# Turning the gated blocks of a SwiGLU as 32x32 squares, with the moves between quadrants on SyncE's DMA queue

## The chip, the cores and the metric

One core of one Trainium2 chip runs the whole kernel. The metric is the device time of one execution, in microseconds (us).

## The reference

A decoder trunk of two layers over x of 256 rows and 2048 columns, all float32. Each layer adds a token mixer (layer 0: chunked gated linear attention, layer 1: forgetting softmax attention), and then a SwiGLU:

```python
h = rms_norm(x, norm_ffn[i])
x = x + (jax.nn.silu(h @ w_gate[i]) * (h @ w_up[i])) @ w_down[i]    # w_gate, w_up: 2048 x 5632, w_down: 5632 x 2048
```

The change lies in the two SwiGLU stages.

## The kernel before, in words

**Products.** Every large product is float32 made of float32r products: a weight chunk (256 rows x 512 columns, 512 KB, as 128 partitions x 1024) is split into a high and a low part, and TensorE adds hi x hi, lo x hi and hi x lo (three matmuls of 512 columns for each 128x128 block of the left side). A chunk takes 12 matmuls.

**The path of a chunk.** SyncE loads it into `raw` (L332, four slots); it waits until the chunk four before has its low part. ScalarE makes `w_hi` (L766) once the chunk has landed and TensorE is through with the chunk four before; VectorE makes `w_lo` = raw - w_hi (L1244); TensorE waits for `w_lo` and multiplies. The four engines each have their own program, with the order written out by hand; semaphores count chunks.

**Gate and up.** `DFF` = 5632 is worked in 11 tiles (`FT`) of 512 columns. A plain tile i (i = 0, 1, 2 and 10) takes 8 chunks of `w_gate` (n = 0 to 7) and then 8 of `w_up` (n = 8 to 15). Tiles 3 to 9 (`gate_up`, from `GU0` to `GU1`) have 16 chunks as well, and one pair of chunks in them (n = 6 and 7) goes through a seven-product scheme: VectorE makes differences of the raw chunks, ScalarE and VectorE split them, TensorE makes seven products for eight, and VectorE adds them up again (`g_sum`). ScalarE then makes the silu of the gate product into `act`; early in tile i+1, after the third chunk, VectorE multiplies it with the up product into `stage` (`hidden`, `hidden_joined`): a gated block, 128 partitions x 2 row blocks x 512.

**Turning a gated block.** The down projection needs it with its columns on the partitions. `swap_h` (L1295) does this with VectorE: 16 transposes (L1304), each from 32 partitions of `stage` to 32 partitions of `hraw` (`ht_raw` in the trace), with eight 32x32 squares in each, spread between the `w_lo` of the chunks n = 3 to 12. At n = 14 ScalarE copies `hraw` to `ht_hi` (L878) and VectorE makes `ht_lo` (L1313), both `turn_h`. For the first two blocks `sums` (L1323 to L1326) also forms sums of parts of `hraw` for the seven-product scheme of the down projection. The last block of a layer is turned in the first chunks of the down projection. The attention output tiles use `swap_h` as well, and go on doing so.

**Down.** Two passes of 44 chunks (`ORDER`), with four pairs in the seven-product scheme in each.

Of the kernel before, what the change touches and what calls it, by code (L numbers as in the profile page):

```python
# [37 lines left out]
P = 128  # L38
Q = 32
# [37 lines left out]
def build(nc, x, norm_mix, norm_ffn, gla_w_in, gla_w_g2, gla_b_g2, gla_o_gain, gla_w_o,  # L77
# [59 lines left out]

    def gate_chunk(c_up, i):
        return Lin(c_up + 2 * CH * i) if isinstance(i, int) else Lin(c_up, 2 * CH, i)
# [7 lines left out]
    with ctx:  # L147
# [102 lines left out]
        xt_half = 4 * KC * S // 2  # L250
        g_hi = at("gate_diff_hi", [P, 4, N], 36 * K, F32R)
# [61 lines left out]
        diff_part = sem("first_differences_made")  # L313
        p1_gate, gate_sums, gate_joined, up_joined = (sem("first_gate_product_read"), sem("gate_sums_made"),
# [10 lines left out]
        @block.sync  # L325
        def _(sp):
            def load(src, row, col, c, j):

                slot = j % SLOTS

                wait(sp, lo_done, c + (j - SLOTS + 1))
                sp.dma_start(  # L332
                    raw[:, slot, :].rearrange("p (k n) -> p k n", n=N),
                    src[row:row + KC_CHUNK * P, bass.ds(col, N) if not isinstance(col, int) else slice(col, col + N)]
                    .rearrange("(k p) n -> p k n", p=P)).then_inc(landed[slot], 16)

            def project(src, col0, tiles, c0):

                with sp.Fori(0, tiles // 2) as i:
                    for j in range(2 * CH):  # L340
                        load(src, j % CH * KC_CHUNK * P, i * (2 * N) + (col0 + j // CH * N),
                             Lin(c0, 2 * CH, i), j)

            def swiglu(layer, c_up, c_down):
                plain = [("one", j // CH, j % CH) for j in range(2 * CH)]
                for i in range(FT):
                    for n, (kind, t, j) in enumerate(ORDER_GU if GU0 <= i < GU1 else plain):
                        load((w_gate, w_up)[t][layer], j * KC_CHUNK * P, i * N, gate_chunk(c_up, i), n)
                for i in range(DT // 2):
                    for n, (kind, t, j) in enumerate(ORDER):  # L350
                        load(w_down[layer], j * KC_CHUNK * P, i * (2 * N) + t * N, Lin(c_down + 2 * HCH * i), n)

            def load_x(h):
                s = slice(h * KC_CHUNK * P, (h + 1) * KC_CHUNK * P)
                sp.dma_start(xres[:, :, s], x[0, :, s].rearrange("(b p) n -> p b n", p=P)) \
                    .then_inc(x_landed[h], 16)

            x_before = {0: (0,), 1: (1,), 2: (2,), 3: (3,), 4: (4, 5), 5: (6,), 6: (7,)}
            for j in range(2 * CH):
                for h in x_before.get(j, ()):  # L360
                    load_x(h)
                load(gla_w_in[0], j % CH * KC_CHUNK * P, j // CH * N, Lin(C["gla_in"]), j)
            project(gla_w_in[0], 2 * N, 2 * QT + 2 * DT - 2, C["gla_in"] + 2 * CH)
            project(gla_w_o[0], 0, DT, C["gla_o"])
            swiglu(0, C["ffn0"], C["down0"])
            project(fox_w_in[0], 0, 3 * DT, C["fox_in"])
            project(fox_w_in[0], 3 * D + FH, DT, C["fox_in"] + 3 * DT * CH)
            project(fox_w_o[0], 0, DT, C["fox_o"])
            swiglu(1, C["ffn1"], C["down1"])
            for b in range(TB):  # L370
                sp.wait_ge(staged, G["ffn1"] + FT + DT + b)
                sp.dma_start(out[0, b * P:(b + 1) * P, (DT - 1) * N:DT * N], stage[:, b, :]).then_inc(last_stored, 16)
            sp.wait_ge(last_stored, 16 * TB)
# [378 lines left out]
        def _(ac):  # L752
# [122 lines left out]
            def turn_h(n, t):  # L875

                wait(ac, turned, n + 1)
                nc.scalar.activation(ht_hi[:, bass.ds(t.v * 4, 4), :] if t.reg is not None  # L878
                                     else ht_hi[:, 4 * t.base:4 * t.base + 4, :],
                                     hraw[:, :, :], ACT.Copy).then_inc(tp_hi, 1)  # L880
# [30 lines left out]
            def out_and_ffn(c_o, g_o, c_up, g_up, c_down, g_down, norm, first, first_turn, after):  # L911
# [6 lines left out]

                def silu(i):
                    count = i if isinstance(i, int) else 0  # L920
                    reg = i is not None and not isinstance(i, int)
                    wait(ac, chunk_used, Lin(c_up + CH, 2 * CH, i) if reg else Lin(c_up + (2 * count + 1) * CH))

                    wait(ac, staged, Lin(g_up, 1, i) if reg else Lin(g_up + count))
                    if i is None:
                        ac.wait_ge(rstd_ready, norm + 1)
                    for b in range(TB):
                        last = nc.scalar.activation(act[:, b, :], acc[:, 0, b, :], ACT.Silu,
                                                    scale=rstd[:, norm, b:b + 1])
                    last.then_inc(gate_done, 1)  # L930
# [3 lines left out]
                for i in range(1, 1 + SEVEN // 2):  # L934
                    cc = Lin(c_up + i * 2 * CH)
                    tile(cc, 0, None)
                    tile(cc, CH, lambda: silu(i), lambda: turn_h(Lin(g_up - 1 + i), Lin(i - 1)))
# [11 lines left out]
                gate_up(layer, c_up, GU0, lambda: silu_joined(GU0), lambda: turn_h(Lin(g_up - 1 + GU0), Lin(GU0 - 1)))  # L949
                with ac.Fori(GU0 + 1, GU1) as i:  # L950
                    gate_up(layer, c_up, i, lambda: silu_joined(i), lambda: turn_h(Lin(g_up - 1, 1, i), Lin(-1, 1, i)))
                for i in range(GU1, FT):
                    cc = Lin(c_up + i * 2 * CH)
                    tile(cc, 0, None)
                    tile(cc, CH, lambda: silu(i), lambda: turn_h(Lin(g_up - 1 + i), Lin(i - 1)))
                events = {(0, 10): lambda: turn_h(Lin(g_up + FT - 1), Lin(FT - 1))}
# [275 lines left out]
        def _(ve):  # L1232
# [76 lines left out]
            def turn_h(n, t):  # L1309
                wait(ve, turned, n + 1)  # L1310
                wait(ve, tp_hi, n + 1)
                s = bass.ds(t.v * 4, 4) if t.reg is not None else slice(4 * t.base, 4 * t.base + 4)
                nc.vector.tensor_tensor(ht_lo[:, s, :], hraw[:, :, :], ht_hi[:, s, :].bitcast(F32),  # L1313
                                        ALU.subtract).then_inc(tp_lo, 1)

            def sums(i):

                src = hraw[:, :, :].rearrange("p (j r) (b t) -> p j r b t", r=KC_CHUNK, t=P)
                a11, a12, a21, a22 = (src[:, :, r, b, :] for b in range(TB) for r in range(KC_CHUNK))
                dst = s_raw[i % (SEVEN // 2)]  # L1320
                if i >= SEVEN // 2:
                    ve.wait_ge(diff_used, down_step(i // (SEVEN // 2) - 1, DT // 2 - 1, SEVEN - 1) + 1)
                nc.vector.tensor_tensor(dst[:, :, 2, :], a11, a21, ALU.subtract)  # L1323
                link(nc.vector.tensor_tensor(dst[:, :, 0, :], a21, a22, ALU.add))
                link(nc.vector.tensor_tensor(dst[:, :, 1, :], dst[:, :, 0, :], a11, ALU.subtract))
                nc.vector.tensor_tensor(dst[:, :, 3, :], a12, dst[:, :, 1, :], ALU.subtract).then_inc(sum_raw, 1)  # L1326
# [27 lines left out]
            def gate_up(layer, c_up, i, hidden, turn, swap):  # L1354
# [4 lines left out]
                for n, (kind, t, j) in enumerate(ORDER_GU):  # L1359
# [26 lines left out]
                    if n in (3, 4, 5, 8, 9, 10, 11, 12):  # L1386
                        swap(2 * (n - 3) if n < 6 else 2 * (n - 5))
# [4 lines left out]
                    if n == 13:  # L1392
                        wait(ve, gate_sums, sums + 1)
# [98 lines left out]
            def out_and_ffn(c_o, g_o, c_up, g_up, c_down, g_down, m, norm, first, first_turn, saved):  # L1492
# [31 lines left out]
                def gate_swaps(n):  # L1524
                    return lambda j: swap_h(n, 2 * (j - 3), 2) if j >= 3 else None

                def up_swaps(n):
                    return lambda j: swap_h(n, 10 + 2 * j, 2) if j < 3 else None

                tile(Lin(c_up), 2 * CH, lambda: hidden(Lin(0)), swaps=gate_swaps(Lin(g_up)))  # L1530
                layer = norm // 2

                def turn_sums(n, i):
                    turn_h(n, Lin(i))
                    sums(layer * (SEVEN // 2) + i)

                tile(Lin(c_up), 3 * CH, None, lambda: turn_sums(Lin(g_up), 0), swaps=up_swaps(Lin(g_up)))
                x_sums_low(layer)
                for i in range(2, 1 + SEVEN // 2):
                    sums_lo(layer * (SEVEN // 2) + i - 2)  # L1540
                    n = Lin(g_up - 1 + i)
                    tile(Lin(c_up + i * 2 * CH), 0, lambda: hidden(Lin(i - 1)), swaps=gate_swaps(n))
                    tile(Lin(c_up + i * 2 * CH), CH, None, lambda: turn_sums(n, i - 1), swaps=up_swaps(n))
                sums_lo(layer * (SEVEN // 2) + SEVEN // 2 - 1)
                def hidden_joined(i):
# [9 lines left out]
                    for b in range(TB):  # L1555
# [5 lines left out]
                gate_up(layer, c_up, GU0, lambda: hidden(Lin(GU0 - 1)), lambda: turn_h(Lin(g_up - 1 + GU0), Lin(GU0 - 1)),  # L1561
                        lambda first: swap_h(Lin(g_up - 1 + GU0), first, 2))
                with ve.Fori(GU0 + 1, GU1) as i:
                    gate_up(layer, c_up, i, lambda: hidden_joined(i), lambda: turn_h(Lin(g_up - 1, 1, i), Lin(-1, 1, i)),
                            lambda first: swap_h(Lin(g_up - 1, 1, i), first, 2))
                for i in range(GU1, FT):
                    cc = Lin(c_up + 2 * CH * i)
                    n = Lin(g_up - 1 + i)
                    tile(cc, 0, lambda: hidden_joined(i) if i == GU1 else hidden(Lin(i - 1)), swaps=gate_swaps(n))
                    tile(cc, CH, None, lambda: turn_h(n, Lin(i - 1)), swaps=up_swaps(n))  # L1570
# [7 lines left out]
                swapped(g_up + FT - 1, 0, (3, 4, 5, 8))  # L1578
                events[0, 11] = lambda: turn_h(Lin(g_up + FT - 1), Lin(FT - 1))
# [500 lines left out]
```

## Time and profile before

| | |
|---|---|
| median of 3 runs | 2296.45 us (2296.32 to 2296.54) |
| profiled execution, its own time | 2296.2 us |
| its span, first to last instruction | 2294.5 us |
| TensorE matmul busy | 2287.3 us |
| VectorE busy | 1725.1 us (75%) |
| ScalarE busy | 1153.3 us (50%) |
| DMA engines, mean busy share by SyncE's queue | 63.7% |
| granted TensorE clock | 1.00 of full speed |

Busy is the time in which an engine runs at least one instruction. For matmuls it is modelled, and neighbouring ones overlap: a matmul of 512 columns is shown with 0.39 us, but they follow each other every 0.23 us. In the timeline a row gives the start in us from the span's start, the time from there to the end of the last of the xN instructions, the engine, the line, the operation and what it writes and reads; the bracket says how long the engine was idle before and for whom. SPq and ACTq are SyncE's and ScalarE's own queues, which issue DMAs; PEld is TensorE's weight load.

### The profile page before, as it was taken

The page shows a single profiled execution, that of the slowest core. Times are in us where ns is not written, and L with a number is a line of the kernel's source. Part 1 is how long each engine was busy: PE and PEld are TensorE (multiplying, and loading weights), DVE is VectorE, ACT ScalarE, POOL GpSimd, SP SyncE. Part 2 cuts the span into 40 slices and gives each one's busy share as a digit, 9 for nine tenths or more (in the row PEclk, how much of TensorE's full clock was granted, in tenths as well). Part 3 has the DMA queues.
Part 4 walks back from the last instruction along what each step waited for, and adds up shares of the span by engine and source line. Part 5 has one row for each costly group of instructions (what it writes and reads, how often), then busy time and mean ns, then how long its engine had stood idle before and what let it go on. Part 6 is the DMA issues. An engine that isn't in the chain of part 4 may idle for free.

```text
span 2294.5 us, 28139 instructions
## 1 busy us (share of the span) xinstructions
PE 2287.3 (100%) x10326; PEld 1895.5 (83%) x10326; DVE 1725.1 (75%) x2151; ACT 1153.3 (50%) x1471; POOL 167.1 (7%) x206
## 2 busy tenths in 40 slices
PE   9999999999999999999999999999999999999999
PEld 7888788888888888888888888888888888888887
DVE  6888468678888887887578755577678888878575
ACT  5545554444445444454566656445444544545343
POOL 2036110000000000000222200001000000000000
PEclk9999999999999999999999999999999999999999
DMA  7655545666666666665768876656666666666664
GB/s 218 190 176 158 172 157 183 206 189 196 198 199 192 194 195 201 195 200 199 190 165 218 204 190 153 158 177 201 192 194 194 198 193 199 193 197 198 215 204 150
DMA packets 229950, 436.03 MB, mean 190 GB/s; under 512 B 17604, under 2 KB 19752, under 8 KB 229848
## 3 DMA queue, kind: packets, MB, share of 16 engines
q1 hardware_dynamic: 224416, 430.49, 63.7%
q0 software_dynamic: 1040, 3.69, 0.4%
q8 instruction: 62, 1.02, 0.2%
q10 hardware_dynamic: 4392, 0.50, 0.2%
q14 instruction: 40, 0.33, 0.0%
HBM read 432.52 MB, written 2.11 MB: 189 GB/s over the span
## 4 chain that ended last, share of the span: by engine, by line
PE 98%; DVE 1%; ACT 1%; issue 0%; ACTq 0%; POOL 0%; POOLq 0%; DVEq 0%
PE acc L418 16%; PE acc L420 16%; PE acc L419 16%; PE acc L428 14%; PE acc L429 14%; PE acc L427 14%; PE wk L646 1%; PE wk L428 1%; PE wk L427 1%; PE tp L428 1%; PE tp L427 1%; PE wk L429 1%; PE tp L429 1%; DVE w_lo L1244 0%; PE tp L385 0%; PE wk L703 0%
## 5 line engine op out<-in xcount | busy, mean ns | idle before, releaser
L766 ACT ACTIVATE w_hi<-raw 128x1024 fp32r<-128x1024 f32 x786 | 823.6, 1060 | 846.8 <-PE acc L429 451.5
L1244 DVE TENSOR_TENSOR w_lo<-raw,w_hi 128x1024 fp32r<-128x1024 f32 x786 | 971.7, 1250 | 367.7 <-ACT w_hi L766 363.3
L418 PE MATMUL acc<-w_hi,xt_hi 128*128 128x512 f32 x1408 | 554.3, 394 | 2.2 <-DVE w_lo L1244 2.1
L420 PE MATMUL acc<-w_hi,xt_lo 128*128 128x512 f32 x1408 | 548.3, 389 | 0.0
L419 PE MATMUL acc<-w_lo,xt_hi 128*128 128x512 f32 x1408 | 548.0, 389 | 0.0
L418 PEld LDWEIGHTS acc<-w_hi,xt_hi 128*128 128x128 f32 x1408 | 264.4, 188 | 60.5 <-issue 3.2
L427 PE MATMUL acc<-w_hi,xt_hi 128*128 128x512 f32 x798 | 310.4, 389 | 0.0
L428 PE MATMUL acc<-w_lo,xt_hi 128*128 128x512 f32 x798 | 310.4, 389 | 0.0
L429 PE MATMUL acc<-w_hi,xt_lo 128*128 128x512 f32 x798 | 310.4, 389 | 0.0
L420 PEld LDWEIGHTS acc<-w_hi,xt_lo 128*128 128x128 f32 x1408 | 264.3, 188 | 55.5
L419 PEld LDWEIGHTS acc<-w_lo,xt_hi 128*128 128x128 f32 x1408 | 264.5, 188 | 54.4 <-issue 1.0
L427 PE MATMUL acc<-w_hi,ht_hi 128*128 128x512 f32 x592 | 230.3, 389 | 0.0
L428 PE MATMUL acc<-w_lo,ht_hi 128*128 128x512 f32 x592 | 230.3, 389 | 0.0
L429 PE MATMUL acc<-w_hi,ht_lo 128*128 128x512 f32 x592 | 230.3, 389 | 0.0
L1304 DVE STREAM_TRANSPOSE ht_raw<-stage 32x256 f32<-32x256 f32 x496 | 216.1, 436 | 9.4
L427 PEld LDWEIGHTS acc<-w_hi,xt_hi 128*128 128x128 f32 x798 | 149.8, 188 | 31.1
L428 PEld LDWEIGHTS acc<-w_lo,xt_hi 128*128 128x128 f32 x798 | 149.8, 188 | 31.1
L429 PEld LDWEIGHTS acc<-w_hi,xt_lo 128*128 128x128 f32 x798 | 149.8, 188 | 31.0
L427 PEld LDWEIGHTS acc<-w_hi,ht_hi 128*128 128x128 f32 x592 | 111.1, 188 | 23.1
L428 PEld LDWEIGHTS acc<-w_lo,ht_hi 128*128 128x128 f32 x592 | 111.1, 188 | 23.0
L429 PEld LDWEIGHTS acc<-w_hi,ht_lo 128*128 128x128 f32 x592 | 111.1, 188 | 23.0
L418 PE MATMUL acc<-w_hi,yt_hi 128*128 128x512 f32 x256 | 99.9, 390 | 0.0
(315 smaller groups left out, 1982.4 us busy)
## 6 DMA issues: line engine op xcount, KB each, us to landing
raw<-in_ffn_w_gate_dram SPq DMA_DIRECT2D x176, 512.0 KB, 4.2
raw<-in_ffn_w_up_dram SPq DMA_DIRECT2D x176, 512.0 KB, 4.2
raw<-in_ffn_w_down_dram SPq DMA_DIRECT2D x176, 512.0 KB, 4.3
raw<-in_fox_w_in_dram SPq DMA_DIRECT2D x128, 512.0 KB, 5.5
raw<-in_gla_w_in_dram SPq DMA_DIRECT2D x96, 512.0 KB, 4.5
raw<-in_gla_w_o_dram SPq DMA_DIRECT2D x32, 512.0 KB, 4.0
raw<-in_fox_w_o_dram SPq DMA_DIRECT2D x32, 512.0 KB, 4.1
xres<-in_x_dram SPq DMA_DIRECT2D x8, 256.0 KB, 6.6
```

Of the source, the lines that this page charges most:

```text
L418: pe.matmul(o, xh, wh, start=(k == 0), stop=False)
L419: pe.matmul(o, xh, wl, start=False, stop=False)
L420: last = pe.matmul(o, xl, wh, start=False, stop=(k == chunks * KC_CHUNK - 1))
L427: pe.matmul(o, xh, wh, start=start, stop=False)
L428: pe.matmul(o, xh, wl, start=False, stop=False)
L429: return pe.matmul(o, xl, wh, start=False, stop=stop)
L646: last = pe.matmul(wk[:, b, h * P:(h + 1) * P], ks, qs, start=(kf == 0), stop=(kf == FPH - 1))
L766: nc.scalar.activation(w_hi[:, slot, :], raw[:, slot, :], ACT.Copy).then_inc(hi_done, 1)
L1244: nc.vector.tensor_tensor(w_lo[:, slot, :], raw[:, slot, :], w_hi[:, slot, :].bitcast(F32), ALU.subtract).then_inc(lo_done, 1)
L1304: last = nc.vector.transpose(dst[32 * j:32 * j + 32, :, :, 32 * i:32 * i + 32], src[32 * i:32 * i + 32, :, :, 32 * j:32 * j + 32])
```

## The change

`swap_h` is no longer used for gated blocks. In its place, after the chunk n = 3, VectorE does two transposes (`squares_h`), one for each row block: all 128 partitions x 512 of `stage` at once, each 32x32 square turned inside its quadrant of partitions, into `ht_sq`, which lies over `act`. Then SyncE issues 16 DMAs of 32 partitions x 1 KB (`move`), which take square (i, j) from quadrant i of `ht_sq` to quadrant j of `hraw`. In SyncE's program they stand right behind the load of chunk n = 7, ahead of that of n = 8, behind waits for the transposes, for the last reads of `hraw`, and for the sums where these read `hraw`. A semaphore `moved` counts 256 for each block. `hraw` now holds its columns in another order, so that the readers (`turn_h` on ScalarE and VectorE, `sums`) take it in runs of 32 elements. `turn_h` waits for `moved` in place of `turned`. Because `ht_sq` lies over `act`, whoever writes `act` next (ScalarE's silu, and VectorE's sum in `gate_up`) waits for the moves too.

```diff
+        ht_sq = act[:, :, :].rearrange("p b n -> p (b n)").rearrange("p (j f) -> p j f", j=4)
+        HQ = hraw[:, :, :].rearrange("p i (e c) -> p e i c", c=Q)
...
+                def move(t):
+                    n = g_up + t
+                    sp.wait_ge(turned, n + 1)
+                    sp.wait_ge(tp_hi, n)
+                    sp.wait_ge(tp_lo, n)
+                    if t == 0:
+                        sp.wait_ge(x_sum_raw, layer + 1)
+                    elif t <= SEVEN // 2:
+                        sp.wait_ge(sum_raw, layer * (SEVEN // 2) + t)
+                    for i in range(4):
+                        for j in range(4):
+                            sp.dma_start(hraw[Q * j:Q * j + Q, i, :], ht_sq[Q * i:Q * i + Q, j, :]) \
+                                .then_inc(moved, 16)
...
                         load((w_gate, w_up)[t][layer], j * KC_CHUNK * P, i * N, gate_chunk(c_up, i), n)
+                        if i and n == CH - 1:
+                            move(i - 1)
...
                         load(w_down[layer], j * KC_CHUNK * P, i * (2 * N) + t * N, Lin(c_down + 2 * HCH * i), n)
+                        if i == 0 and n == CH - 1:
+                            move(FT - 1)
...
-                wait(ac, turned, n + 1)
-                nc.scalar.activation(ht_hi[:, bass.ds(t.v * 4, 4), :] if t.reg is not None
-                                     else ht_hi[:, 4 * t.base:4 * t.base + 4, :],
-                                     hraw[:, :, :], ACT.Copy).then_inc(tp_hi, 1)
+                wait(ac, moved, (t + (layer * FT + 1)) * 256)
+                dst = ht_hi[:, bass.ds(t.v * 4, 4), :] if t.reg is not None else ht_hi[:, 4 * t.base:4 * t.base + 4, :]
+                nc.scalar.activation(dst.rearrange("p k (b i c) -> p (k b) i c", b=TB, c=Q), HQ,
+                                     ACT.Copy).then_inc(tp_hi, 1)
...
+                    wait(ac, moved, gate_tile(layer, i or 0) * 256)
                     for b in range(TB):
                         last = nc.scalar.activation(act[:, b, :], acc[:, 0, b, :], ACT.Silu,
...
+            def squares_h(n):
+                wait(ve, staged, n + 1)
+                dst = ht_sq.rearrange("p j (k b c) -> p b k j c", b=TB, c=Q)
+                for b in range(TB):
+                    last = nc.vector.transpose(dst[:, b], stage[:, b, :].rearrange("p (k j c) -> p k j c", j=4, c=Q))
+                last.then_inc(turned, 1)
...
-                    if n in (3, 4, 5, 8, 9, 10, 11, 12):
-                        swap(2 * (n - 3) if n < 6 else 2 * (n - 5))
+                    if n == 3:
+                        swap()
...
                     if n == 13:
+                        wait(ve, moved, gate_tile(layer, i) * 256)
                         wait(ve, gate_sums, sums + 1)
...
-                swapped(g_up + FT - 1, 0, (3, 4, 5, 8))
+                events[0, 3] = lambda: squares_h(Lin(g_up + FT - 1))
```

## Rows read from the trace of the kernel before

**Rows 1.** Page, head and first part: busy us, share of span, instructions.

```profile
span 2294.5 us, 28139 instructions
PE 2287.3 (100%) x10326; PEld 1895.5 (83%) x10326; DVE 1725.1 (75%) x2151; ACT 1153.3 (50%) x1471; POOL 167.1 (7%) x206
```

**Rows 2.** Waits of TensorE over the whole span: us in total, times, longest.

```profile
PE acc L418 <- DVE w_lo L1244: 2.1, 4, 1.0
PE wk L585 <- POOL ident L1954: 1.6, 1, 1.6
```

**Rows 3.** Windows: busy us by engine in a loop tile, and in the down projection.

```profile
569.00:612.00 43.00, 43.00 (x191) 35.61 (x191) 37.68 (x46) 21.11 (x22) 0.00 (x0) 1.00 0.66 198
870.00:940.00 70.00, 70.00 (x310) 57.98 (x310) 56.70 (x62) 34.16 (x32) 0.00 (x0) 1.00 0.61 193
```

**Rows 4.** Groups of VectorE by shape: busy us, mean ns of one, idle before.

```profile
L1304 DVE STREAM_TRANSPOSE ht_raw<-stage 32x256 f32<-32x256 f32 x496 | 216.1, 436 | 9.4
...
L1390 DVE TENSOR_TENSOR gate_product_sums<-wk,gate_product_sums 128x512 f32<-128x512 f32 x14 | 9.7, 692 | 0.4
...
L1325 DVE TENSOR_TENSOR sum_raw<-sum_raw,ht_raw 128x256 f32<-128x256 f32 x4 | 1.7, 425 | 0.1
```

**Rows 5.** Timeline of layer 0's tile 5, several short windows.

```profile
621.57 1.22 DVE L1244 TENSOR_TENSOR w_lo<-raw,w_hi 128x1024 fp32r<-128x1024 f32 x1
...
622.81 0.37 SPq L332 DMA_DIRECT2D raw<-in_ffn_w_up_dram  x1
...
624.84 0.37 SPq L332 DMA_DIRECT2D raw<-in_ffn_w_gate_dram  x1
...
632.48 1.07 ACT L766 ACTIVATE w_hi<-raw 128x1024 fp32r<-128x1024 f32 x1
...
634.77 1.22 DVE L1244 TENSOR_TENSOR w_lo<-raw,w_hi 128x1024 fp32r<-128x1024 f32 x1
...
639.54 0.19 PEld L427 LDWEIGHTS acc<-w_hi,xt_hi 128*128 128x128 f32 x1
...
647.70 0.68 DVE L1394 TENSOR_TENSOR gate_product_sums<-wk,gate_product_sums 128x512 f32<-128x512 f32 x1
```

**Rows 6.** Timeline of the first 7 us: issues on SyncE's and ScalarE's queues.

```profile
0.82 0.44 SPq L355 DMA_DIRECT2D xres<-in_x_dram  x1
1.32 0.46 SPq L332 DMA_DIRECT2D raw<-in_gla_w_in_dram  x1
...
3.36 0.90 SPq L332 DMA_DIRECT2D raw<-in_gla_w_in_dram  x1
4.30 0.55 SPq L355 DMA_DIRECT2D xres<-in_x_dram  x1
...
6.22 0.40 ACTq L979 DMA_DIRECT2D grow<-in_norm_ffn_dram  x1
...
6.65 0.59 ACTq L979 DMA_DIRECT2D grow<-in_gla_o_gain_dram  x1
```

**Rows 7.** DMA: SyncE's queue in total; issues with KB and us to landing.

```profile
q1 hardware_dynamic: 224416, 430.49, 63.7%
...
raw<-in_ffn_w_up_dram SPq DMA_DIRECT2D x9, 512.0 KB, 3.9
...
out_dram<-stage SPq DMA_DIRECT2D x2, 256.0 KB, 2.2
```

**Rows 8.** Timeline of a plain tile and of the down projection's start.

```profile
448.73 0.37 SPq L332 DMA_DIRECT2D raw<-in_ffn_w_gate_dram  x1
...
467.50 0.19 PEld L418 LDWEIGHTS acc<-w_hi,xt_hi 128*128 128x128 f32 x1
...
879.17 0.37 SPq L332 DMA_DIRECT2D raw<-in_ffn_w_down_dram  x1
...
897.25 0.19 PEld L427 LDWEIGHTS acc<-w_hi,ht_hi 128*128 128x128 f32 x1
```

More of the change, by code:

```diff
@@ L136, in gate_count, with gate_tile @@
         return Lin((base + i) * per) if isinstance(i, int) else Lin(base * per, per, i)
+    def gate_tile(layer, i):
+        return Lin(layer * FT + i) if isinstance(i, int) else Lin(layer * FT, 1, i)
     def gate_chunk(c_up, i):
@@ L313, in build @@
         diff_part = sem("first_differences_made")
+        moved = sem("squares_moved")
         p1_gate, gate_sums, gate_joined, up_joined = (sem("first_gate_product_read"), sem("gate_sums_made"),
@@ L344, in swiglu @@
             def swiglu(layer, c_up, c_down):
+                g_up = G[f"ffn{layer}"]
+                def move(t):
[11 more added lines that the diff above has]
+                                .then_inc(moved, 16)
                 plain = [("one", j // CH, j % CH) for j in range(2 * CH)]
@@ L873, in turn_x, with turn_h @@
                 last.then_inc(tp_hi, 1)
-            def turn_h(n, t):
-                wait(ac, turned, n + 1)
-                nc.scalar.activation(ht_hi[:, bass.ds(t.v * 4, 4), :] if t.reg is not None
-                                     else ht_hi[:, 4 * t.base:4 * t.base + 4, :],
-                                     hraw[:, :, :], ACT.Copy).then_inc(tp_hi, 1)
+            def turn_h(layer, n, t):
+                wait(ac, moved, (t + (layer * FT + 1)) * 256)
+                dst = ht_hi[:, bass.ds(t.v * 4, 4), :] if t.reg is not None else ht_hi[:, 4 * t.base:4 * t.base + 4, :]
+                nc.scalar.activation(dst.rearrange("p k (b i c) -> p (k b) i c", b=TB, c=Q), HQ,
+                                     ACT.Copy).then_inc(tp_hi, 1)
             def turn_y(n, t, gain):
@@ L917, in out_and_ffn @@
                          swapped_tile=(lambda: turn_x(g_o + t - 1, gain, t - 1, hraw)) if t else None)
+                layer = int(g_down is None)
                 def silu(i):
@@ L936, in out_and_ffn @@
                     tile(cc, 0, None)
-                    tile(cc, CH, lambda: silu(i), lambda: turn_h(Lin(g_up - 1 + i), Lin(i - 1)))
+                    tile(cc, CH, lambda: silu(i), lambda: turn_h(layer, Lin(g_up - 1 + i), Lin(i - 1)))
                     sums_hi(layer * (SEVEN // 2) + i - 1)
@@ L947, in silu_joined @@
                     last.then_inc(gate_done, 1)
-                gate_up(layer, c_up, GU0, lambda: silu_joined(GU0), lambda: turn_h(Lin(g_up - 1 + GU0), Lin(GU0 - 1)))
+                gate_up(layer, c_up, GU0, lambda: silu_joined(GU0), lambda: turn_h(layer, Lin(g_up - 1 + GU0), Lin(GU0 - 1)))
                 with ac.Fori(GU0 + 1, GU1) as i:
-                    gate_up(layer, c_up, i, lambda: silu_joined(i), lambda: turn_h(Lin(g_up - 1, 1, i), Lin(-1, 1, i)))
+                    gate_up(layer, c_up, i, lambda: silu_joined(i), lambda: turn_h(layer, Lin(g_up - 1, 1, i), Lin(-1, 1, i)))
                 for i in range(GU1, FT):
@@ L954, in out_and_ffn @@
                     tile(cc, 0, None)
-                    tile(cc, CH, lambda: silu(i), lambda: turn_h(Lin(g_up - 1 + i), Lin(i - 1)))
-                events = {(0, 10): lambda: turn_h(Lin(g_up + FT - 1), Lin(FT - 1))}
+                    tile(cc, CH, lambda: silu(i), lambda: turn_h(layer, Lin(g_up - 1 + i), Lin(i - 1)))
+                events = {(0, 10): lambda: turn_h(layer, Lin(g_up + FT - 1), Lin(FT - 1))}
                 for pp in range(DT // 2):
@@ L1307, in swap_h, with turn_h @@
                     last.then_inc(turned, 1)
-            def turn_h(n, t):
-                wait(ve, turned, n + 1)
+            def squares_h(n):
[4 more added lines that the diff above has]
+                last.then_inc(turned, 1)
+            def turn_h(layer, n, t):
+                wait(ve, moved, (t + (layer * FT + 1)) * 256)
@@ L1311, in turn_h @@
                 wait(ve, tp_hi, n + 1)
                 s = bass.ds(t.v * 4, 4) if t.reg is not None else slice(4 * t.base, 4 * t.base + 4)
-                nc.vector.tensor_tensor(ht_lo[:, s, :], hraw[:, :, :], ht_hi[:, s, :].bitcast(F32),
-                                        ALU.subtract).then_inc(tp_lo, 1)
+                hi, low = (h[:, s, :].rearrange("p k (b i c) -> p (k b) i c", b=TB, c=Q) for h in (ht_hi, ht_lo))
+                nc.vector.tensor_tensor(low, HQ, hi.bitcast(F32), ALU.subtract).then_inc(tp_lo, 1)
@@ L1316, in sums @@
             def sums(i):
-                src = hraw[:, :, :].rearrange("p (j r) (b t) -> p j r b t", r=KC_CHUNK, t=P)
-                a11, a12, a21, a22 = (src[:, :, r, b, :] for b in range(TB) for r in range(KC_CHUNK))
-                dst = s_raw[i % (SEVEN // 2)]
+                src = hraw[:, :, :].rearrange("p i (j r b c) -> p r b j i c", r=KC_CHUNK, b=TB, c=Q)
+                a11, a12, a21, a22 = (src[:, r, b] for b in range(TB) for r in range(KC_CHUNK))
+                dst = s_raw[i % (SEVEN // 2)][:, :, :, :].rearrange("p j d (i c) -> p d j i c", c=Q)
@@ L1321, in sums @@
                 if i >= SEVEN // 2:
                     ve.wait_ge(diff_used, down_step(i // (SEVEN // 2) - 1, DT // 2 - 1, SEVEN - 1) + 1)
[L1323 to L1326, printed above, removed]
+                nc.vector.tensor_tensor(dst[:, 2], a11, a21, ALU.subtract)
@@ L1328, in sums_lo @@
+                link(nc.vector.tensor_tensor(dst[:, 0], a21, a22, ALU.add))
+                link(nc.vector.tensor_tensor(dst[:, 1], dst[:, 0], a11, ALU.subtract))
+                nc.vector.tensor_tensor(dst[:, 3], a12, dst[:, 1], ALU.subtract).then_inc(sum_raw, 1)
             def sums_lo(i):
@@ L1522, in out_and_ffn, with squares @@
                 tile(Lin(c_up), CH, mid=lambda: x_sums(norm // 2))
[L1524 to L1530, printed above, removed]
+                def squares(n):
+                    return lambda j: squares_h(n) if j == 3 else None
+                tile(Lin(c_up), 2 * CH, lambda: hidden(Lin(0)), swaps=squares(Lin(g_up)))
                 layer = norm // 2
                 def turn_sums(n, i):
-                    turn_h(n, Lin(i))
+                    turn_h(layer, n, Lin(i))
                     sums(layer * (SEVEN // 2) + i)
-                tile(Lin(c_up), 3 * CH, None, lambda: turn_sums(Lin(g_up), 0), swaps=up_swaps(Lin(g_up)))
+                tile(Lin(c_up), 3 * CH, None, lambda: turn_sums(Lin(g_up), 0))
                 x_sums_low(layer)
@@ L1541, in out_and_ffn @@
                     n = Lin(g_up - 1 + i)
-                    tile(Lin(c_up + i * 2 * CH), 0, lambda: hidden(Lin(i - 1)), swaps=gate_swaps(n))
-                    tile(Lin(c_up + i * 2 * CH), CH, None, lambda: turn_sums(n, i - 1), swaps=up_swaps(n))
+                    tile(Lin(c_up + i * 2 * CH), 0, lambda: hidden(Lin(i - 1)), swaps=squares(n))
+                    tile(Lin(c_up + i * 2 * CH), CH, None, lambda: turn_sums(n, i - 1))
                 sums_lo(layer * (SEVEN // 2) + SEVEN // 2 - 1)
@@ L1559, in hidden_joined @@
                     last.then_inc(staged, 1)
-                gate_up(layer, c_up, GU0, lambda: hidden(Lin(GU0 - 1)), lambda: turn_h(Lin(g_up - 1 + GU0), Lin(GU0 - 1)),
-                        lambda first: swap_h(Lin(g_up - 1 + GU0), first, 2))
+                gate_up(layer, c_up, GU0, lambda: hidden(Lin(GU0 - 1)), lambda: turn_h(layer, Lin(g_up - 1 + GU0), Lin(GU0 - 1)),
+                        lambda: squares_h(Lin(g_up - 1 + GU0)))
                 with ve.Fori(GU0 + 1, GU1) as i:
-                    gate_up(layer, c_up, i, lambda: hidden_joined(i), lambda: turn_h(Lin(g_up - 1, 1, i), Lin(-1, 1, i)),
-                            lambda first: swap_h(Lin(g_up - 1, 1, i), first, 2))
+                    gate_up(layer, c_up, i, lambda: hidden_joined(i), lambda: turn_h(layer, Lin(g_up - 1, 1, i), Lin(-1, 1, i)),
+                            lambda: squares_h(Lin(g_up - 1, 1, i)))
                 for i in range(GU1, FT):
@@ L1568, in out_and_ffn @@
                     n = Lin(g_up - 1 + i)
-                    tile(cc, 0, lambda: hidden_joined(i) if i == GU1 else hidden(Lin(i - 1)), swaps=gate_swaps(n))
-                    tile(cc, CH, None, lambda: turn_h(n, Lin(i - 1)), swaps=up_swaps(n))
+                    tile(cc, 0, lambda: hidden_joined(i) if i == GU1 else hidden(Lin(i - 1)),
+                         swaps=squares(n))
+                    tile(cc, CH, None, lambda: turn_h(layer, n, Lin(i - 1)))
                 events = {}
@@ L1577, in out_and_ffn @@
                 events[0, 2] = lambda: hidden(Lin(FT - 1))
-                swapped(g_up + FT - 1, 0, (3, 4, 5, 8))
-                events[0, 11] = lambda: turn_h(Lin(g_up + FT - 1), Lin(FT - 1))
+                events[0, 3] = lambda: squares_h(Lin(g_up + FT - 1))
+                events[0, 11] = lambda: turn_h(layer, Lin(g_up + FT - 1), Lin(FT - 1))
                 for pp in range(DT // 2):
```

## The prediction

> **What bounds the kernel now.** I began with the first part of the page [rows 1]: TensorE is busy for 2287.3 of the 2294.5 us, VectorE for 75%. VectorE's high share says nothing about time yet, so next came the waits of TensorE [rows 2]: 2.1 us for VectorE's `w_lo` in the whole span, plus 1.6 us at the start for the identity. The windows over one gated block of the loop and over the first part of the down projection [rows 3] show TensorE busy for every one of 43 and 70 us, while VectorE is busy for 37.68 and 56.70. So in the stretch that the change touches TensorE never stands still, and relief of VectorE has no wait to shorten there. What the change can do is make TensorE wait, if a weight chunk comes late. The rest is therefore a count of slack.
>
> **The transposes.** A gated block is turned today by 16 transposes of 436 ns [rows 4], 6.98 us of VectorE. Two of 128x512 take their place. The trace has no such transpose. The nearest rows: a tensor_tensor of 256 elements per partition takes 425 ns and one of 512 takes 692 [rows 4], and the 256-element transpose (436) lies where the 256-element tensor_tensor lies; so 0.70 us each if the four quadrants run together, 1.4 us for two. The upper bound takes the quadrants one after another: the slope (692-425)/256 = 1.04 ns per element, 4 x 512 of them, plus 0.16 us, is 2.3 us each, 4.6 us for two. I take 1.4: today's 436 ns for 256 elements leaves 0.16 us beside that slope, so one quadrant runs an element of each of its 32 partitions per step, and nothing in the row says that others must wait. Over 22 gated blocks (11 in each of two layers) VectorE loses 22 x (6.98 - 1.4) = 123 us of work. By rows 2 and 3 this is worth nothing to the end. The split and the sums (L878, L1313, L1323 to L1326) keep their count and elements and get access in runs of 32; at worst they take a little longer once per block, far from any edge.
>
> The Trainium skill (Vector Engine (DVE) Microarchitecture Reference, section 3.8) has the transposing front end "sustain one element per cycle per lane". The 436 ns row agrees for one quadrant; no row here shows four at once. By that rule the two cost 1.4 us.
>
> **The 16 transfers on SyncE's queue.** They stand after the issue of chunk 7's load, and chunk 8's load and all later ones stand behind them. Their waits: `turned` (the two transposes, just after the third `w_lo` that chunk 7's load waits for too), and the old reads of `ht_raw`, long done. So SyncE's wait is the 1.4 us of the transposes. Then 16 issues. The queue's issues today: a load of 256 rows every 0.51 us in the first burst (0.82 to 1.32), the one with 32 rows, as a move has, 0.40 us, the next starting 0.43 after it (6.22 to 6.65) [rows 6]. I take 0.44 per issue by that nearest row, 7.0 us for 16. Bounds: 0.37, the duration of a load issued after a wait [rows 5], without any gap, and 0.94, the pitch of the sixth issue of the burst (3.36 to 4.30) [rows 6], where several loads lay in the queue unfinished.
>
> Now one block in the loop, with times of [rows 5]. The chunk-3 `w_lo` ends at 621.57 + 1.22 = 622.79 and chunk 7's load is issued at 622.81. Changed: the transposes end at 624.2, the moves are issued from 624.3 to 631.3, and chunk 8's load goes out at 631.35 instead of 624.84: 6.5 us late. It lands 3.9 us later (median of the up matrix's loads, [rows 7]) at 635.25; its `w_hi` began at 632.48, now at 635.3, takes 1.06, `w_lo` 1.22, together to 637.6. TensorE takes up chunk 8 at 639.54. So the late load is absorbed: 1.9 us remain of 639.54 - (634.77 + 1.22) = 3.55. Chunks 9 to 11 go out back to back behind it at about 0.45 us, each has 2.7 us more of TensorE's time, and one load of 0.524 MB, of the 430.49 MB that this queue moves in 63.7% of the span, takes 0.637 x 2294.5 x 0.524 / 430.49 = 1.8 us of all the DMA engines [rows 7], so they are less tight. Later loads wait for `w_lo` again and the lateness is used up before the block ends. With p for the time per issue, TensorE begins to stall at p = 0.44 + 1.9/16 = 0.56 us per issue.
>
> The other places are wider. In a plain block (chunk 7's load at 448.73) chunk 8 would be ready at 448.73 + 1.5 + 7.0 + 3.9 + 2.3 = 463.4; TensorE takes it at 467.50 [rows 8]: 4.1 left. In the down projection (879.17) it is 893.9 against 897.25 [rows 8]: 3.3 left, and VectorE, which has the seven-product differences there, is rid of 16 transposes in the same stretch. There are 7 loop-type blocks per layer, 14 of the tight sort.
>
> **The moved squares.** 16 moves carry 512 KB, one load's worth, so at most 1.8 us of the DMA engines per block, 22 x 1.8 = 40 us of shared time under a DMA that is busy 64% [rows 7]. A small store on this queue lands in 2.2 us [rows 7]; the last move lands at about 633.5. The first who needs it is VectorE's new wait before the sum at 647.70 [rows 5]: 14 us to spare. Behind that wait stand `act`, the silu, and chunk 14's `w_lo`; behind ScalarE's wait in the split stands chunk 15's `w_hi`. None waits. The new semaphore waits cost instructions of tens of ns.
>
> **Sum.** Removed from the path 0, added 0: the profiled execution's 2296.2 stays, and so does the median 2296.45, 0.25 above it. Forecast 2296.4, no change.
>
> **The rivals.**
> (A) SyncE's issues decide, slower. The mechanism is chunk 8's load behind 16 issues in the 14 tight blocks; it decides above p = 0.56. At p = 0.70, say, the stall is 16 x (0.70 - 0.56) = 2.2 us in each, 31 us in all, 2327; at 0.60, 9 us, 2305; at the bound 0.94, 6.1 us x 14 = 85, and in the 6 plain blocks 16 x (0.94 - 0.44) - 4.1 = 3.9 each and the 2 down ones 4.7 each, 33 more, 2414. For it: one issue of the burst took 0.90 [rows 6], and SyncE will have load 7 and 16 moves behind one another. Against: those slow issues came with loads of 256 rows, a move has an eighth of them. Chance 0.15.
> (B) The transposes run quadrant after quadrant: 4.6 us instead of 1.4, everything 3.2 later, 3.2 - 1.9 = 1.3 us stall x 14 = 18 us, 2315. Nothing in the trace speaks for it. Chance 0.06.
> (C) The moves don't overlap: each pays its landing, 2.2 us, before the next, 35 us per block, and chunk 8's load is stuck behind them, ready at 624.3 + 35.2 + 3.9 + 2.3 = 665.7, 26 us late. About 22 x 26 = 570 us, near 2870. Against: the loads in the burst follow each other at half a microsecond while each needs several to land. Chance 0.02.
> The Trainium skill (DMA: Bandwidth & Descriptors, Rules for kernel authors) says of many small transfers that below 64 KB one pays mostly overhead; a move is 32 KB. By that rule at its strictest (C) would hold; no row shows transfers so small in a row on this queue. The page also puts the fixed 2 us mostly into completion, which successive transfers can share, and the burst agrees.
> (D) VectorE's relief is worth something after all: it would have to cut into the waits of [rows 2], which lie outside the gated blocks, or speed up TensorE itself. If all 2.1 us went, 2294.3. More than that needs a cause that I don't see. Chance of over 0.2%: 0.04.
>
> **How the numbers follow.** 0.2% is 4.6 us, about what a measurement of this kernel can tell from no change. No change holds 0.73; (A), (B) and (C) together 0.23, all slower; (D) 0.04. A small part of (A), p up to 0.58, gives under 4.6 us and is counted as no change. The range goes from the 2.1 us of (D) with some measuring error, 2293.5, up to (A) at about p = 0.60, 2306; beyond it lie (B), (C) and two thirds of (A), about 0.17, and below it about 0.03.
>
> **What would show it.** In the changed profile: VectorE's busy time down by about 120 us to 1600; a transpose row x44 at 0.70; 16 issues at 0.44 us, from 1.5 us after chunk 7's load; chunk 8's load 6.5 us later than today relative to chunk 7's; a DMA wait of ScalarE's `w_hi` of about 3 us per loop block, new; TensorE's waits still about 4 us. Wrong if TensorE shows waits for `w_lo` at chunk 8 or 9 of the loop blocks: then the issue pitch or the transpose is longer than I took.

## The result and the profile after

The changed kernel takes 2312.44 us (median; 2311.67 to 2314.57) against 2296.49 in the same session: ratio 1.0072, 95% interval 1.0059 to 1.0085. It is 16 us slower; forecast was no change, with a range up to 2306. The profiled execution is the slowest of the four (2314.57 us); its span is 2312.9 us, 18.4 more than before, so the trace shows about 2 us more loss than the median has. Head and first part of the page after, against [rows 1]:

```profile
span 2312.9 us, 28204 instructions
## 1 busy us (share of the span) xinstructions
PE 2294.3 (99%) x10326; PEld 1895.0 (82%) x10326; DVE 1600.1 (69%) x1843; ACT 1153.0 (50%) x1471; POOL 168.0 (7%) x206
```

VectorE lost 125 us of work, and the kernel became slower. The waits of TensorE (us in total, times, longest), against [rows 2], have a new row:

```profile
PE acc L454 <- DVE w_lo L1274: 10.6, 13, 1.9
PE acc L445 <- DVE w_lo L1274: 1.9, 4, 1.0
PE wk L612 <- POOL ident L1991: 1.6, 1, 1.6
PE tp L605 <- DMA xres<-in_x_dram: 0.6, 1, 0.6
PE tp L454 <- DVE diff_lo L1497: 0.4, 2, 0.2
```

L454 is the first matmul of a weight block in the loop tiles and the down projection, L445 in the plain tiles (L427 and L418 before). These rows count from the modelled end of the matmul before, and leave out slower matmuls afterwards, so they add up to less than the time that was lost. TensorE waits for VectorE, but VectorE is not the cause: one step back, in ScalarE's waits,

```profile
ACT w_hi L793 <- DMA raw<-in_ffn_w_gate_dram: 83.5, 14, 7.2
ACT w_hi L793 <- DMA raw<-in_ffn_w_up_dram: 72.5, 88, 7.1
```

ScalarE stands 14 times, once for each loop tile, 6 us on average, for a chunk of `w_gate` that has not landed: chunk n = 8, the only one of `w_gate` behind the moves there. The chain that ended last says the same: SyncE's queue, absent before, holds 6% of it (first line before, second after).

```profile
PE 98%; DVE 1%; ACT 1%; issue 0%; ACTq 0%; POOL 0%; POOLq 0%; DVEq 0%
PE 83%; SPq 6%; DVE 4%; DMA 3%; issue 2%; ACT 1%; ACTq 0%; DVEq 0%
```

The same tile as in [rows 5], after (timeline; the times are about 4.4 us later than before, for the stalls ahead of it):

```profile
626.00 1.22 DVE L1274 TENSOR_TENSOR w_lo<-raw,w_hi 128x1024 fp32r<-128x1024 f32 x1
627.13 1.30 DVE L1344 STREAM_TRANSPOSE act<-stage 128x512 f32<-128x512 f32 x2
...
627.24 0.37 SPq L338 DMA_DIRECT2D raw<-in_ffn_w_up_dram  x1
628.46 10.23 SPq L365 DMA_DIRECT2D ht_raw<-act  x16
638.73 0.58 SPq L338 DMA_DIRECT2D raw<-in_ffn_w_gate_dram  x1
...
642.99 1.06 ACT L793 ACTIVATE w_hi<-raw 128x1024 fp32r<-128x1024 f32 x1 [6.37 <-DMA raw<-in_ffn_w_gate_dram]
...
644.09 2.50 DVE L1274 TENSOR_TENSOR w_lo<-raw,w_hi 128x1024 fp32r<-128x1024 f32 x2 [5.14 <-ACT w_hi L793]
...
645.37 0.50 PE L454 MATMUL acc<-w_hi,xt_hi 128*128 128x512 f32 x1 [1.02 <-DVE w_lo L1274]
```

Read it from the `w_lo` that ends at 627.22. The transposes are done for the first move at 628.46. The 16 issues last until chunk 8's load goes out at 638.73: 10.27 us, 0.64 each. The load has landed at 642.99, `w_hi` and `w_lo` follow without a pause, and TensorE takes chunk 8 at 645.37, where the distance of before (639.54 - 622.79 = 16.75 behind that `w_lo`) would be 643.97. All 352 moves together (duration of an issue in ns, least, median and most; the next one starts some 40 ns after it ends):

```profile
L365 SPq DMA_DIRECT2D ht_raw<-act x352: 507/591/1837, 450.5 to 2088.2; - x176
```

From one first weight load of a tile to the next, the tiles 4 to 9 of both layers took 42.84 us before and now 43.7 to 44.2, one 46.65; tile 3 just holds (its chunk 8 is ready 0.1 to 0.4 us ahead), the plain tiles lose 0.0 to 0.1 us each. All tiles and down passes together take 17.8 us more. That is the whole of the 18.4 but 0.6, which lies in the first 10 us.

### The profile page after: what moved, and what is told of

It is laid out like the page before. It is cut to its first block, busy times and chain, and to the rows that moved or that the text cites. A ratio compares the mean times of both kernels' runs of the same rounds, so it can differ in the third digit from the quotient of the medians.

```text
span 2312.9 us, 28204 instructions
## 1 busy us (share of the span) xinstructions
PE 2294.3 (99%) x10326; PEld 1895.0 (82%) x10326; DVE 1600.1 (69%) x1843; ACT 1153.0 (50%) x1471; POOL 168.0 (7%) x206
## 4 chain that ended last, share of the span: by engine, by line
PE 83%; SPq 6%; DVE 4%; DMA 3%; issue 2%; ACT 1%; ACTq 0%; DVEq 0%
PE acc L445 16%; PE acc L447 16%; PE acc L446 16%; PE acc L454 10%; PE acc L456 10%; PE acc L455 10%; SPq L365 6%; DMA raw<-in_ffn_w_gate_dram 2%; DVE w_lo L1274 1%; ACT w_hi L793 1%; DMA raw<-in_ffn_w_down_dram 1%; PE wk L673 1%; DVE gate_product_sums L1586 1%; DVE act L1344 0%; PE tp L412 0%
## 5 line engine op out<-in xcount | busy, mean ns | idle before, releaser
L445 PE MATMUL acc<-w_hi,xt_hi 128*128 128x512 f32 x1408 | 554.4, 394 | 2.1 <-DVE w_lo L1274 1.9
L454 PE MATMUL acc<-w_hi,xt_hi 128*128 128x512 f32 x798 | 312.7, 392 | 9.9 <-DVE w_lo L1274 9.9
L445 PEld LDWEIGHTS acc<-w_hi,xt_hi 128*128 128x128 f32 x1408 | 264.4, 188 | 60.5 <-DVE w_lo L1274 3.3
L454 PE MATMUL acc<-w_hi,ht_hi 128*128 128x512 f32 x592 | 230.4, 389 | 0.7 <-DVE w_lo L1274 0.7
L454 PEld LDWEIGHTS acc<-w_hi,xt_hi 128*128 128x128 f32 x798 | 150.1, 188 | 46.1 <-DVE w_lo L1274 15.0
L454 PEld LDWEIGHTS acc<-w_hi,ht_hi 128*128 128x128 f32 x592 | 111.1, 188 | 23.9 <-DVE w_lo L1274 1.1
L445 PE MATMUL acc<-w_hi,yt_hi 128*128 128x512 f32 x256 | 99.9, 390 | 0.0
L447 PE MATMUL acc<-w_hi,yt_lo 128*128 128x512 f32 x256 | 99.6, 389 | 0.0
```

The lines of the kernel that those rows point to most:

```text
L445: pe.matmul(o, xh, wh, start=(k == 0), stop=False)
L447: last = pe.matmul(o, xl, wh, start=False, stop=(k == chunks * KC_CHUNK - 1))
L454: pe.matmul(o, xh, wh, start=start, stop=False)
```

## The experiments

Theory 1: SyncE's time for 16 issues in a row holds back chunk 8's load beyond the slack. Rival 2: the transfers themselves disturb the loads, in the DMA engines or in SBUF. Rival 3: the new order of the squares, or the new waits, slow ScalarE and VectorE.

### e1_spread: four moves behind each of four loads

```diff
-                        if i and n == CH - 1:
-                            move(i - 1)
+                        if i and CH - 1 <= n < CH + 3:
+                            move(i - 1, n - (CH - 1))
```

(the second argument picks the four moves with i = n - 7; the down projection in the same way)

> The changed kernel with its 16 moves put in four groups of four, behind the loads of chunks n = 7, 8, 9 and 10 instead of all behind n = 7. Same transposes, same 16 transfers, same bytes. Theory 1 (the time that SyncE needs to issue 16 moves in a row, 0.64 us each, holds back chunk 8's load until TensorE runs dry): a load is now held back by 4 issues at most, 2.6 us, less than the 7 us of slack; no stall, 2296.5, ratio to before 1.000. Rival (the transfers disturb the loads in the DMA engines, or the new order of the squares slows the splits): unchanged at about 2312, ratio 1.007.

Measured: 2296.20 us, ratio 1.0000 (0.9991 to 1.0009). All tiles take their 42.84 us again. Same transfers, same order of squares, same two transposes, same waits: rival 3 would have stayed, and rival 2 too unless it needs the 16 transfers in one row. In the timeline each load now stands behind four issues only:

```profile
624.27 2.41 SPq L366 DMA_DIRECT2D ht_raw<-act  x4
626.73 0.58 SPq L338 DMA_DIRECT2D raw<-in_ffn_w_gate_dram  x1
627.35 2.41 SPq L366 DMA_DIRECT2D ht_raw<-act  x4
629.80 0.58 SPq L338 DMA_DIRECT2D raw<-in_ffn_w_up_dram  x1
```

### e2_pool: GpSimd issues the moves

```diff
-                            sp.dma_start(hraw[Q * j:Q * j + Q, i, :], ht_sq[Q * i:Q * i + Q, j, :]) \
+                            po.dma_start(hraw[Q * j:Q * j + Q, i, :], ht_sq[Q * i:Q * i + Q, j, :]) \
                                 .then_inc(moved, 16)
```

(with the same waits, in GpSimd's program between `x_rstd(1)` and the saves of the down projection, and behind `x_rstd(3)`)

> The changed kernel with the 16 moves issued by GpSimd instead of SyncE. SyncE's program is that of before. Theory 1: the loads go out as before, no stall from SyncE; GpSimd's issues of before took 0.6 to 0.85 us each, so 16 take 10 to 14 us from 1.5 us after chunk 3's w_lo, and the squares are needed 25 us after it: in time. 2296.5, ratio 1.000. If the DMA engines or SBUF were what is contended: about 2312, as the same transfers run in the same stretch.

Measured: 2296.16 us, ratio 1.0000 (0.9991 to 1.0010). The 16 transfers run in the same stretch of the tile, SyncE is free, and nothing is lost: rival 2 falls. GpSimd's issues:

```profile
L2028 POOL DMA_DIRECT2D ht_raw<-act x352: 496/496/761, 450.1 to 2072.6; - x176
```

0.50 us each (min, median and max in ns), less than I expected; a move lands 3.6 us after it, against 1.9 from SyncE's queue.

### e3_n12 and e3_n24: 12 and 24 issues in place of 16

```diff
                         for j in range(4):
+                            if 4 * i + j < 12:
...
+                            pieces = 2 if 4 * i + j < 8 else 1
+                            for h in range(pieces):
+                                c = slice(h * (S // pieces), (h + 1) * (S // pieces))
```

(the first for 12, the others for 24: eight of the moves in two halves; the waits for `moved` count 192 and 384 for each block in place of 256)

> The changed kernel with 12 of the 16 moves (four are left out, so that part of each gated block isn't moved). Theory 1: in the changed kernel chunk 8 is ready 1.4 us after TensorE wants it; four issues of 0.64 us fewer make it 1.2 us early, so the stall is gone altogether: 2296.5, ratio 1.000. A cost that is proportional to the number of transfers would leave 12/16 of the 16 us: 2308.5, ratio 1.005.

Measured: 2296.21 us, ratio 1.0000 (0.9991 to 1.0009). Not three quarters of the loss, but nothing: chunk 8's `w_lo` is ready 0.9 to 1.6 us ahead of TensorE in tiles 4 to 9 and 2.6 to 3.0 us in tile 3. The loss has a threshold here, between 12 and 16 issues. This kernel leaves part of each block unmoved, so only its time is read.

> The changed kernel with 24 moves in place of 16: eight of them are cut in two of 512 B per row, the bytes are the same. Theory 1: 8 x 0.64 = 5.1 us more before chunk 8's load, all of it stall, since the slack is used up: 14 loop tiles x (1.2 + 5.1) + 6 plain tiles x 5.1 + 2 down projections x 6 = 131 us, 2427, ratio 1.057. If the bytes moved were what costs: about 2312, ratio 1.007. Proportional to the number of transfers: 24 us, 2320, ratio 1.010.

Measured: 2467.69 us, ratio 1.0747 (1.0731 to 1.0764): 171 us over before where I had worked out 131. The direction is theory 1's alone, as the bytes are the same; the size is 40 us over it. The windows over the loop tiles of layer 0 and layer 1 (busy us of PE, PEld, DVE, ACT, POOL, then the granted clock) show what I had left out:

```profile
520.00:900.00 380.00, 338.37 (x1411) 276.46 (x1412) 238.37 (x232) 159.29 (x161) 0.00 (x0) 0.93 0.57 179
1720.00:2120.00 400.00, 357.52 (x1494) 291.80 (x1493) 238.95 (x235) 162.63 (x164) 0.00 (x0) 0.94 0.56 177
```

The clock was 1.00 in both before and is 0.93 and 0.94 here. From the starts of successive 512-column matmuls: standing time rose by 128 us, which is the 131 expected, and 198 more of them than before follow their neighbour after 0.43 us in place of 0.23, 39 us. 128 + 39 = 167 of the 171.

### e5_late: the 16 moves of a loop tile behind chunk 11's load

```diff
-                        if i and n == CH - 1:
+                        if i and n == (CH + 3 if GU0 <= i < GU1 else CH - 1):
```

> The changed kernel with all 16 moves of a loop tile behind chunk 11's load in place of chunk 7's; plain tiles and the down projection unchanged. Theory 1: the same 10.3 us of issues now hold back chunk 12's load: due at 636.02 in the rows of before and chunk 11's issue at 632.34, it goes out at about 643.1, lands at 647.3, ready at 649.7 against TensorE's 650.4, so no stall or a few tenths of a us in the 14 loop tiles; the plain tiles and down lose their 2 to 3 us as in the changed kernel: 2299, ratio 1.001, at most 1.003. If 16 issues in a row cost the same wherever they stand: 2312, ratio 1.007.

Measured: 2299.18 us, ratio 1.0013 (1.0003 to 1.0022). The loop tiles take 42.84 us again (two of 14 take 0.03 and 0.14 more), with the same 16 issues in one row:

```profile
632.08 10.23 SPq L365 DMA_DIRECT2D ht_raw<-act  x16
642.36 2.13 SPq L338 DMA_DIRECT2D raw<-in_ffn_w_up_dram  x4
```

What is left, about 3 us, is mostly in the down projections (1.5 and 0.6 us, against 1.6 and 0.7 in the changed kernel) and in the last plain tile of each layer (0.4 and 0.2). So it is not the issues as such that cost, but that they stand where the next load has too little slack.

### e6_dram: five issues by way of HBM

```diff
+                    wait(sp, moved, Lin(64 * block))
+                    sp.dma_start(parked, ht_sq[:, :, :]).then_inc(parked_done, 16)
+                    sp.wait_ge(parked_done, 16 * (block + 1))
+                    for j in range(4):
+                        sp.dma_start(hraw[Q * j:Q * j + Q, :, :],
+                                     parked[:, j, :].rearrange("(i q) f -> q i f", q=Q)).then_inc(moved, 16)
```

(the waits for `moved` count 64 for each block)

> The changed kernel with the squares parked in HBM: one store of all 128 partitions x 4 KB, a wait for it, and four loads, one for each destination quadrant, in place of the 16 moves; still all behind chunk 7's load on SyncE's queue. Twice the bytes, 5 issues instead of 16. Theory 1 (issue time decides): 1.2 us for the transposes, about 0.5 for the store's issue, 3 to 4 for its landing, four issues of 0.46: chunk 8's load goes out about 7 us after chunk 7's in place of 11.5 and the slack holds it; no stall, 2296.5, ratio 1.000. Rival (traffic of the transfers in the DMA engines costs): twice the traffic, and in HBM, so more than 2312, ratio over 1.007.

Measured: 2296.19 us, ratio 1.0001 (0.9991 to 1.0010). Twice the traffic and SyncE's wait for a landing in between (3.8 us), and still no loss: in the tile shown above chunk 8's load goes out 6.7 us behind chunk 7's in place of 11.5. Rival 2 falls a second time.

### e4_shapes and e7_kinds: what an issue costs

```diff
+            group(0, [(hraw[Q * j:Q * j + Q, i, :], flat[Q * i:Q * i + Q, j * S:j * S + S]) for i, j in cells])
...
+            group(6, [(hraw[Q * j:Q * j + Q, i, :], w_down[0][Q * (4 * i + j):Q * (4 * i + j) + Q, 0:S]) ...
```

> The kernel before, and behind its last store nine groups of DMAs on SyncE's idle queue, each group issued in a row and then waited for: (0) the 16 moves; (1) eight moves that stay in their quadrant; (2) four of 128 partitions x 1 KB; (3) eight of 4 partitions x 1 KB; (4) eight of 16 partitions x 1 KB; (5) eight of 32 partitions x 128 B; (6) eight of 32 rows x 1 KB from HBM; (7) four weight loads of 256 rows x 2 KB; (8) eight of 32 partitions x 4 KB. Only the issue times count; the total grows by some 70 us. Theory 1a (the issue costs by the shape of the transfer: a one-dimensional list of few rows is dearer for the queue than a weight load): about 0.63 us per issue in (0), (1), (5), (6), (8), 0.51 in (7), whatever the source. Theory 1b (SBUF as source is what costs): 0.63 in all but (6) and (7), and (6) like the 0.43 that the prediction took. Theory 1c (it was the other work of the kernel that slowed the issues): 0.44 in (0) on the idle chip.

Both kernels of this part ran once each (2356.49 and 2321.8 us), and only the times of their issues are read. In the trace, from start to start within a group, past its first two:

```
group                              rows x bytes       us per issue
0, 1  SBUF to SBUF                 32 x 1 KB          0.633
2     SBUF to SBUF                 128 x 1 KB         0.644
3     SBUF to SBUF                 4 x 1 KB           0.620
4     SBUF to SBUF                 16 x 1 KB          0.632
5     SBUF to SBUF                 32 x 128 B         0.633
8     SBUF to SBUF                 32 x 4 KB          0.633
6     HBM to SBUF                  32 x 1 KB          0.464
7     HBM to SBUF (weight load)    256 x 2 KB         0.514
```

The timeline merges them; the first row is groups 0 to 5 with their waits in between, the second is group 6:

```profile
2293.98 38.95 SPq L379 DMA_DIRECT2D ht_raw<-act  x52
2334.05 3.61 SPq L379 DMA_DIRECT2D ht_raw<-in_ffn_w_down_dram  x8
2339.16 1.93 SPq L379 DMA_DIRECT2D raw<-in_ffn_w_down_dram  x4
2347.57 4.97 SPq L379 DMA_DIRECT2D raw<-raw  x8
```

This is theory 1b: between two places in SBUF neither rows nor bytes matter (0.62 to 0.64 throughout), and 32 rows of 1 KB cost 0.46 once they come from HBM. Theories 1a and 1c fall: the shape is the same in groups 0 and 6, and it is 0.63 on an otherwise idle chip too. For loads from HBM the shape does count a little: 0.464 against the weight load's 0.514.

> The kernel before, and behind its last store more bursts on the idle queues: (0) eight stores of 32 partitions x 1 KB from SBUF to HBM; (1) eight copies of 32 x 1 KB within HBM; (2) eight transfers that are by turns from HBM and from SBUF, into SBUF; (3) eight moves SBUF to SBUF on SyncE's queue while ScalarE's queue issues eight of its own. Theory 1b1 (both sides in SBUF is what costs): 0.46 in (0) and (1), 0.63 for the SBUF ones alone in (2). Theory 1b2 (SBUF as the source costs): 0.63 in (0), 0.46 in (1). In (3) 0.63 on each queue if each pays for itself, about twice that if they share what makes the lists.

```profile
2294.18 3.58 SPq L383 DMA_DIRECT2D far<-act  x8
2298.94 5.05 SPq L383 DMA_DIRECT2D far<-in_ffn_w_down_dram  x8
```

Eight stores SBUF to HBM take 3.58 us (0.464 from start to start), eight copies HBM to HBM 5.05 us (0.633). So SBUF as the source is not it, nor SBUF as both ends in particular: of 32 rows of 1 KB, an issue with both ends in the same kind of memory costs 0.633 us, one from the one to the other 0.464. Neither of the two forms of theory 1b had the HBM copies right. By turns (group 2) the issues come every 0.55 to 0.62 us, so the two prices don't simply alternate: a load from HBM right behind a move takes 0.58 us, as chunk 8's load does behind the moves in the changed kernel. With ScalarE's queue issuing eight of its own at once, SyncE keeps 0.63 to 0.64 (eight in 4.96 us) and ScalarE has 0.64 to 0.65 but for one: each pays for itself, nothing is shared.

## Why the prediction was wrong

**The slack, and TensorE as the bound: right.** No wait of TensorE could be shortened, and none was: with the loss removed (e1, e2, e3_n12, e6) the time is that of before within 0.1%, with VectorE 125 us lighter (123 forecast). (D) had nothing to find.

**The transposes: right.** 1.4 us for two with all four quadrants at once; the row after reads

```profile
L1344 DVE STREAM_TRANSPOSE act<-stage 128x512 f32<-128x512 f32 x44 | 28.6, 687 | 0.0
```

0.69 each, and the first move went out 1.24 us after the `w_lo`. (B), quadrant after quadrant, is out. Against the 436 ns of 256 elements in one quadrant this is (687 - 436) / 256 = 0.98 ns per element with four quadrants at once, close to the slope of 1.04 that I had taken. The Trainium skill (Vector Engine (DVE) Microarchitecture Reference, section 3.8) has one element per cycle per lane; the trace agrees in that four quadrants take no longer per element than one, while no run here shows how long a cycle is.

**The issue of a move: the step that failed.** I took 0.44 us "by that nearest row", the one with 32 rows, 7.0 us for 16; it took 0.64, 10.3 us for 16, and that lies above the 0.56 at which the slack ends. That row was near by its number of rows, which e4 shows to be of no weight between two places in SBUF, and far by its ends: it was a load from HBM, and for such a load it was nearly right (0.464 in e4). A move has both ends in SBUF, for which the trace of before has no row. It was also a row of ScalarE's queue, where I had written "the queue's issues"; that did no harm, as moves cost 0.64 to 0.65 us there (e7). The bounds, 0.37 and 0.94, did hold the value; that (A), everything above 0.56, got a chance of only 0.15 came from "a move has an eighth of them", an argument from the number of rows that no row had shown. So the 0 that the sum adds to the path should have been some 16 us, nearly all of it TensorE's wait for late chunks.

**The consequence of it: right in kind and nearly in size.** (A) said where (chunk 8's load), in which tiles (the 14), and from which point: 0.56 us per issue. Put 0.64 in: 16 x 0.08 = 1.3 us x 14 = 18 us; measured 16.0 by the medians, and 17.8 by the tiles of the profiled execution, the slowest of four. That they agree so well is in part luck. In the profiled execution 12 tiles lose and not 14, since in tile 3 of each layer chunk 8 is still in time, 11 of the 12 lose 0.8 to 1.3 us, and the twelfth 3.8, and the two down projections make up the rest. The other terms of the working: the landing took 4.26 us in place of 3.9 (0.2 of it because the load behind the moves is itself issued in 0.58 us instead of 0.37), and the transposes gave 0.2 back. The plain tiles lost little (at most 0.11 us each), also as worked out; the down projections lost 1.6 and 0.7 us where at 0.64 the working gives 0.1 to spare. In layer 0 one of the 16 issues took 1.68 us, and TensorE stood about 1 us for chunk 8. The rest was not in the working at all: it followed the delay to chunk 8 only, but some 13 us later TensorE loses another 0.5 us in layer 0 and 0.6 in layer 1, in the next seven-product pair, mostly because its `diff_lo` comes late (the row of `PE tp L454` above).

**(C), moves that don't overlap: out.** They land 1.9 us after their issue each, and the next is issued 0.63 after it. Of the rule against small transfers (Trainium skill, DMA: Bandwidth & Descriptors, Rules for kernel authors) these runs agree with the mere warning, and not with the strict reading behind (C): 32 KB take 0.63 us of the queue that issues them, a weight load of 512 KB takes 0.37 to 0.51. What cost time here was this overhead of the issuing queue; the same transfers cost nothing when GpSimd issued them (e2). The same page of the Trainium skill, section "Issuing engines are not separate DMA queues", calls the time to initiate a DMA "usually small relative to the DMA itself"; here 16 of them took 10.3 us for one load's worth of bytes.

**What stays open.** Why an issue with both ends in the same kind of memory is dearer. What made four of the 352 issues take 0.94 to 1.84 us isn't shown either, but the trace has a hint: the four start at 457.5, 584.3, 893.4 and 1729.2 us, and the queue `q8 instruction`, which has 62 packets in the whole execution, has one of 16 KB at 457.2, 584.4, 893.3 and 1728.3, and none between the first and the last move of any other block. The four long issues of e3_n12 and of e5_late come with such a packet as well. No run varied it.

## What to carry to other kernels

A queue that issues loads is an engine with a busy time of its own: count what stands between two loads in issues times their duration, and hold it against the slack of the very next load. The loss starts at a threshold (here between 12 and 16 issues), so spread the extra issues over several loads or give them to a queue that has nothing urgent behind it. The bytes did not decide: twice the traffic in five issues cost nothing (e6), and the same bytes in 24 issues cost 171 us (e3_n24). To price an operation that the trace doesn't have, ask first in which respect a row must be like it, and where that isn't known, let the range reach to the row that is unlike in any of them.

## What the runs showed of the hardware

The issue price above: from SBUF to SBUF 0.62 to 0.64 us for 4 to 128 rows and 128 B to 4 KB per row; with 32 rows of 1 KB, 0.633 from HBM to HBM and 0.464 from HBM to SBUF or back; 0.514 for a weight load of 256 rows of 2 KB.

A short stand of TensorE can cost more than its length. In tile 4 of layer 0 one issue took 1.84 us, TensorE stood 2.05 us, and some 1.6 us (six matmuls) after it had gone on the clock fell (windows with the stand, right after it and later, same columns as [rows 3]; 0.62 is a mean of the full 2.4 GHz and the half, 1.2 GHz):

```profile
597.00:600.00 3.00, 1.11 (x6) 0.61 (x5) 1.63 (x2) 2.27 (x3) 0.00 (x0) 1.00 1.05 406
600.00:604.00 4.00, 4.00 (x13) 3.15 (x12) 3.27 (x3) 1.97 (x2) 0.00 (x0) 0.62 0.83 240
604.00:611.00 7.00, 7.00 (x31) 5.75 (x31) 4.75 (x6) 3.67 (x4) 0.00 (x0) 0.98 0.85 269
```

Seven matmuls in a row then took 0.43 us each: 1.4 us on top of 2.05. The order in time is all that this shows; no run varied the length of a stand by itself. None of the other stands in the changed kernel's SwiGLU stages, 0.3 to 1.2 us long, did this. In e3_n24, with a stand of 3.6 to 7.0 us in each of the 22 blocks, 5 to 13 slow matmuls followed each, and they made up 39 of the 171 us.
